# Half A's seven-product stage: the low part of each group's second attention output moved up on VectorE

## What is computed

```python
def swiglu_ffn(h, w_gate, w_up, w_down):
    return (jax.nn.silu(h @ w_gate) * (h @ w_up)) @ w_down      # 1024 -> 2816 -> 1024

...
s = jnp.einsum('bnqkgd,bnskd->bkgnqs', q, k) * SCALE            # 16 query heads, 4 key heads
s = s - alibi_slopes * dist
p = exp(s - m); p = p / (sum(p) + exp(sink - m))
o = jnp.einsum('bkgnqs,bnskd->bnqkgd', p, v)                    # own 64 frames and two chunks back
return o.reshape(B, T, N_HEADS * HEAD_DIM) @ w_o
```

## Time and profile before

| | before |
|---|---|
| median of 3 runs | 2167.36 us (2166.36 to 2167.45) |
| profiled execution, its own time | 2164.6 us |
| its span, first to last instruction | 2162.8 us |
| mean granted TensorE clock | 0.997 |
| PE busy | 2128.5 us, 98% |
| DVE busy | 1538.8 us, 71% |
| POOL busy | 1457.7 us, 67% |
| ACT busy | 1216.8 us, 56% |

### The profile page before, as it was taken

The page is one execution under the profiler, slowest core; times in us unless marked ns, Lnnn a source line. Parts: engine busy times, 40 slices in busy tenths (PEclk is TensorE's granted clock), DMA queues, the critical chain, the costliest instruction groups (busy, mean ns, idle before and its releaser), DMA issues. The chain is left out here.

```text
span 2162.8 us, 38537 instructions
## 1 busy us (share of the span) xinstructions
PE 2128.5 (98%) x14080; PEld 1959.5 (91%) x14080; DVE 1538.8 (71%) x2508; ACT 1216.8 (56%) x2176; POOL 1457.7 (67%) x939
## 2 busy tenths in 40 slices
PE   9899999999999999999999999999999999999999
PEld 8798877888889789999999898989898989999999
DVE  5998788863434578888886458788888447665665
ACT  7556665433424666777763466677777434444443
POOL 3787889976446557676766644767676655868775
PEclk9999999999999999999999999999999999999999
DMA  5112323332333623222234442322223424243232
GB/s 158 49 50 59 88 84 96 98 98 88 98 97 106 136 71 98 79 80 85 77 94 132 134 103 74 92 78 87 79 79 98 123 85 118 89 118 105 83 107 81
DMA packets 316313, 203.07 MB, mean 94 GB/s; under 512 B 42374, under 2 KB 288734, under 8 KB 315486
## 3 DMA queue, kind: packets, MB, share of 16 engines
q1 hardware_dynamic: 314248, 199.49, 31.5%
q10 hardware_dynamic: 1878, 1.11, 0.2%
HBM read 188.72 MB, written 9.42 MB: 92 GB/s over the span
## 5 line engine op out<-in xcount | busy, mean ns | idle before, releaser
L3246 POOL TENSOR_TENSOR wlo<-raw,whi 128x1024 fp32r<-128x1024 f32 x160 | 397.8, 2488 | 319.2 <-PE ps L680 165.7
L3373 POOL TENSOR_TENSOR wlo<-raw,whi 128x512 fp32r<-128x512 f32 x280 | 396.0, 1430 | 227.9 <-ACT whi L2002 212.2
L1546 ACT ACTIVATE whi<-raw 128x1024 fp32r<-128x1024 f32 x160 | 169.3, 1059 | 294.8 <-PE ps L680 161.5
L680 PE MATMUL ps<-hAh,whi 128*128 128x512 f32 x736 | 284.6, 392 | 2.7 <-ACT hAh L1597 0.9
L680 PE MATMUL ps<-hAl,whi 128*128 128x512 f32 x736 | 283.1, 390 | 0.2
L2002 ACT ACTIVATE whi<-raw 128x512 fp32r<-128x512 f32 x280 | 172.5, 627 | 116.8 <-DVE raw L2797 69.8
L3277 POOL TENSOR_TENSOR accp<-accp,prod 128x574 f32<-128x574 f32 (+1 forms) x136 | 192.5, 1415 | 29.6 <-ACT prod L1680 18.3
L2535 DVE TENSOR_TENSOR xB<-ps,xB 128x544 f32<-128x544 f32 x184 | 132.4, 720 | 97.8 <-PE ps L680 41.7
L680 PE MATMUL ps<-hAh,wlo 128*128 128x512 f32 x736 | 187.8, 397 | 0.0
L680 PE MATMUL ps<-hBh,whi 128*128 128x272 f32 x832 | 170.4, 293 | 9.0 <-DVE gxA L2399 3.6
L680 PE MATMUL ps<-hBl,whi 128*128 128x272 f32 x832 | 171.5, 293 | 0.8
(11 more groups left out here) (475 smaller groups left out, 6327.4 us busy)
## 6 DMA issues: line engine op xcount, KB each, us to landing
raw<-in_w_gate_dram SPq DMA_DIRECT2D x80, 256.0 KB, 3.0
raw<-in_w_up_dram SPq DMA_DIRECT2D x80, 256.0 KB, 3.0
raw<-in_w_down_dram SPq DMA_DIRECT2D x80, 256.0 KB, 2.8
raw<-in_w_pw_dram SPq DMA_DIRECT2D x38, 512.0 KB, 3.9
raw<-in_w_gate_dram SPq DMA_DIRECT2D x38, 512.0 KB, 3.8
raw<-in_w_up_dram SPq DMA_DIRECT2D x38, 512.0 KB, 3.9
raw<-in_w_down_dram SPq DMA_DIRECT2D x36, 512.0 KB, 3.5
raw<-in_w_qkv_dram SPq DMA_DIRECT2D x32, 256.0 KB, 3.7
```

What stands on the lines that cost most here:

```text
L680: ins = nc.tensor.matmul(o, wt[n % 2][:, P * k:P * (k + 1)], src[h][:, k, c0:c0 + w], start=start, stop=stop)
L1546: nc.scalar.activation(whi[n % 2][:], raw_of(n)[:], ACT.Copy).then_inc(w_hi, 1)
L3246: nc.gpsimd.tensor_tensor(wlo[n % 2][:], raw_of(n)[:], f(whi[n % 2][:]), ALU.subtract).then_inc(w_lo, 1)
L3373: nc.gpsimd.tensor_tensor(two(S, wlo[t][:, cols]), v_source(S, s), two(S, f(whi[t][:, cols])), ALU.subtract).then_inc(S.lo, 1)
```

## The change

In every group the low part of the second unit's output (`out_low(att, prev, 1)`) is made directly behind that of the first, ahead of the sum of product b of the up matrix. Before, it stood ahead of the last sums of the up matrix, behind `read_scores(att, cur, 3)`. No instruction is added or taken away, and no wait is changed.

```diff
                     v_sum_up(S, "U", G, "d")
                     v_sum_up(S, "U", G, "f")
                     out_low(att, prev, 0)
+                    out_low(att, prev, 1)
                     v_sum_up(S, "U", G, "b")
                     turned_low(att, prev, 3)
                     out_sum(att, prev, 2)
...
                     v_sum_up(S, "U", G, "e")
                     v_times(S, G, "d")
                     read_scores(att, cur, 3)
-                    out_low(att, prev, 1)
                     v_last_sums(S, "U", G)
                     v_times(S, G, "e")
                     out_low(att, prev, 2)
```

## The result

| | before | after |
|---|---|---|
| median | 2167.40 us (2166.36 to 2168.11, 4 runs) | 2155.89 us (2154.67 to 2156.95, 4 runs) |
| ratio after/before | | 0.9950, 95% interval 0.9937 to 0.9962 |
| profiled execution, its own time | 2164.6 us | 2156.95 us |
| its span | 2162.8 us | 2155.1 us |

The changed kernel is faster by 11.5 us between the medians and by 7.65 us between the two profiled executions. The forecast was 8.14 us, 2159.2 us, and its range began at 2157.4 us. So the sum made against the one profiled execution came out within 0.5 us, and the predicted median missed by 3.3 us, on the far side of the range. A second comparison, with more runs of the kernel before, gave 10.0 us (experiment e2): 2156.77 us, still 0.6 us outside, though the 8.14 us lie within its interval of 7.6 to 13.4 us. Why two executions of one kernel tell different sums is the main question of what follows.

A forecast was written before the change was run, and what follows sets the result against it. TensorE, busy 98% of the span, was taken to bound the kernel, so only its waits count. 5.62 + 1.31 + 1.61 - 0.4 = 8.14 us off the median 2167.36 gave 2159.2 us, range 2157.4 to 2163.8.

The forecast's parts named there:

- Which wait ends: TensorE's waits for `v_times` e on line 2845 go; the output projection waits for `v_times` d on line 2838.
- The lock as the cause: Late in four groups, GpSimd's instruction in course locks out `out_low` on VectorE: 1.47 us against 0.41 us.
- The block in the new place: Behind the first `out_low`, the second is blocked by GpSimd, about 1.5 us; sum of b 0.73 us later.
- The charge of 0.4 us for product e: TensorE's product e just in time behind the sum of b: 0.05 us lost in each of groups 2 to 9.
- The last group and the clock: Output projection starts 1.31 us earlier; its first tile keeps the full clock, 1.61 us saved.
- The groups' term: Groups 3, 5, 6 and 7 lose their late wait and run in 37.02 us: 5.62 us saved together.
- ScalarE isn't on the path there: ScalarE's `out_part` of the fourth unit gets `out_low` up to 3 us earlier, worth nothing.
- The clock did not fall: Rival: clock falls all the same behind the projection's shorter wait; 6.5 us saved, 2160.8 us, chance 0.20.
- other supply: Rival: GpSimd's low parts come late at products c to e; 3.6 to 5.4 us saved, chance 0.19.
- that rival: The last sums, one operand in SBUF, are locked out in `out_low`'s stead; 2.9 us saved, 2164.4 us, chance 0.07.
- The slower side: Second `out_low` stays behind two GpSimd operations, product e waits 1.3 us in nine groups; 2170.2 us, chance 0.07.

The follow-up runs named there:

- e2: The changed kernel, unchanged, run again against the kernel before on the same chip: 2156.77 us, ratio 0.9952, 10.0 us saved.
- e3: Against the kernel before, the step moved in the last group alone, at its old place in groups 2 to 9: 2162.97 us, ratio 0.9988.
- e8: The changed kernel plus a useless 128 x 64 subtraction per group between the two last up sums, both operands in SBUF: 2162.21 us, ratio 0.9979.
- e9: The changed kernel plus a useless 128 x 64 subtraction per group between the two last up sums, one operand in PSUM: 2158.26 us, ratio 0.9960.
- e12: The kernel before, unchanged, traced once more to count blocked groups: traced execution 2168.41 us, all seven groups 2 to 8 blocked.
- e4: Against the kernel before, the step moved in groups 2 to 9, at its old place in the last group: 2158.91 us, ratio 0.9958.
- e7: Against the changed kernel, the step put behind `v_times` e in groups 2 to 9, last group as changed: 2165.61 us, ratio 0.9999 to the kernel before.
- e11: The kernel before, unchanged, traced once more to count blocked groups: traced execution 2165.55 us.

## Why the prediction was right or wrong

**Which wait ends.** Right. The waits on line 2845 are gone in after and are there in e3, where the step stays in the groups' late place, and the projection waits on line 2838.

**The lock as the cause.** Right, and shown by e8 against e9 and by group 4 of the first trace and of e12: the same instruction at the same distance takes 0.41 or 1.58 us.

**The block in the new place.** Right in size: 2.00 us for the pair, the sum of b directly behind it, product e just in time. The charge of 0.4 us for product e was of the right size: groups 2 to 7 last 0.39 us more than 37.02 each together, and 0.45 in e2, though it isn't shown that all of it is product e's. Group 8 adds 0.35 us that the sum doesn't have.

**The last group and the clock.** 1.31 us forecast; 1.15 us less from group 9's first down product to the projection, with a wait of 1.55 us where 1.35 to 1.4 was said. The first tile gave 1.57 us where 1.61 was said. Both terms stand, and e3's 3.8 us (interval 0.6 to 4.6) holds them. That the clock would stay was right, in all eight traces with the step moved in the last group: each has a wait of 1.55 us and a first tile of 6.09 to 6.12 us, while the five of before have waits of 2.75 to 3.10 us and tiles of 7.57 to 8.69. The reason given for it was thin: e4 kept the clock behind 2.36 us.

**The groups' term.** Mis-sized, and this is the miss. The prediction read "the four save 5.62 us together", and then closed with "the median stands 2.76 us above that execution, and I take the saving off it". That treats what separates the median from the trace as a constant that the change leaves alone. It was the removed term itself: the five traces of before have 4, 5, 5, 5 and 7 blocked groups, and without their excess they agree within 1.3 us. Their excess is 6.93 us on average, and by the estimate above the median answers to 8.0. The sum is then 6.93 - 0.74 + 1.15 + 1.57 = 8.9 us with the average, and 8.0 - 0.74 + 1.15 + 1.57 = 10.0 with the estimate, against 10.0 in e2. Both are within e2's interval, so that the second fits so closely is partly luck; it leaves out the 1.05 us behind the first tile and the 1.00 us of group 1, which cancel in the two first traces. The sign was there to read: the groups "where the wait doesn't exist" had the same instruction in the same order against the same run of GpSimd. The prediction explained why four were blocked and never asked why groups 2, 4 and 8 were not; the start 3.74 us into a run of 1.26 us apiece would have answered, some hundredths of a microsecond from the border. A range that charges all seven groups (9.0 us in e12, where 5.62 stood) reaches 3.4 us further down, and holds the result.

Two sizes stay loose: the medians stood 11.5 us apart in the first comparison and 10.0 us in e2, and e3 and e4 add up to 3.8 + 7.9 = 11.7 us. Each has an interval of 2 to 3 us to either side, which takes in both, and e4's trace kept the clock as well, so that part of the gain is counted twice there.

**ScalarE.** Wrong in the step "ScalarE isn't on the path there, so this is worth nothing". e7 takes away the late wait of `v_times` e, as the change does, but leaves `out_low` late for `out_part`, and gains nothing in the groups (2165.61 against 2156.77 us in e2). In a blocked group of before the same path is late by 1.47 us, the group's whole excess, hidden in part by the 1.03 us at tile 3. So releasing ScalarE in time is a condition of the gain. The old place as such would allow it: the groups that ran in 37.02 us had the step there, unblocked. The error didn't change the sum, since the 5.62 us were read from the lengths of whole groups.

**The rivals.** The clock did not fall. No other supply became late by the change (the 0.2 us of GpSimd at line 1025 lie ahead of the first moved step). The sums with a PSUM operand were not locked out, but the idea behind that rival, that the late run of GpSimd finds another victim, did come true: the copy of 128 x 8 on line 2572, SBUF to SBUF with one input, takes 1.15 us in group 5 and 0.80 us in others, where it took 0.60 us in the traces of before and 0.17 us free. No wait of TensorE comes of it: `v_times` e behind it still ends 0.13 us ahead of tile 3 in group 5. The slower side, two instructions of GpSimd in one block, was seen in no trace.

## What to carry to other kernels

Before a term of a sum rests on a collision of two engines, read in the trace how far each case lies from its border. Here a step 0.10 us behind the start of GpSimd's instruction was blocked every time, and one within 0.02 us of it went both ways: such a term is a coin, and its share in the median is to be sized by all places where it can fall, and not by those where it fell in one trace. If the runs spread more than the traced execution explains, the difference between median and trace may be the very term that the change removes, and it must not be carried over as a constant. And of a step that is moved, follow each of its waiters to the end: a second waiter can sit right behind the first one's wait without showing a wait of its own. It shows in the trace of before as an instruction that ends just ahead of its waiter (here 0.05 us), and in a run like e7, which cures the first alone.

## What the runs showed of the hardware

- The outcome of the lock at the same distance differs between executions of one program: the same group gave 0.41 us or 1.58 us. Over the five traced executions of before it makes up most of the spread: 3.8 us with it, 1.3 without.
- Two instructions in a row on VectorE, both with two SBUF operands, don't keep the ports between them: the pair took 2.00 us, with an instruction of GpSimd in between, where it takes 0.76 us in e7.
- A copy with a single SBUF input and SBUF output in float32 is blocked too (0.17 us free, 0.60 to 1.15 us blocked, for 128 x 8), and what is blocked first carries the instruction behind it to the border, where it meets the next one.
- The low clock is not fixed by the length of the wait in front: TensorE went to 1.2 GHz behind 1.97 and 2.96 us of idleness in the first trace of before. At the first of these places it stayed at 2.4 GHz behind 1.93 us in after, and behind 1.96 and 1.95 us in e11 and e12, which are the same program; at the second it stayed behind 2.36 us in e4. At the projection the low clock cost 1.5 to 1.6 us in four traces of before and 2.6 us in e12. What decides was not tried.
